# Constant products on TensorE in the eight norms of a two-block transformer kernel

## What is computed

```python
def _rmsnorm(x, g, eps=RMS_EPS):
    x32 = x.astype(jnp.float32)
    y = x32 * lax.rsqrt(jnp.mean(x32 * x32, axis=-1, keepdims=True) + eps)
    return (y * g.astype(jnp.float32)).astype(x.dtype)
...
h = rms_norm(x, norm_mlp[i]) * (1 + scale2) + shift2
x = x + gate2 * (jnp.square(jax.nn.relu(h @ mlp_w1[i])) @ mlp_w2[i])
```

## Time and profile before

| | |
|---|---|
| median of 3 runs | 3437.49 us (3431.79 to 3440.21) |
| the profiled execution, its own time | 3443.7 us |
| its span, first to last instruction | 3441.6 us |
| mean granted TensorE clock | 0.969 |
| busy share of the span: TensorE, VectorE, ScalarE, GpSimd | 94%, 57%, 36%, 37% |

### The profile page before, as it was taken

The page is one execution under the profiler, slowest core; times in us unless marked ns, Lnnn a source line. Parts: engine busy times, 40 slices in busy tenths (PEclk is TensorE's granted clock), DMA queues, the critical chain, the costliest instruction groups (busy, mean ns, idle before and its releaser), DMA issues.

```text
span 3441.6 us, 60644 instructions
## 1 busy us (share of the span) xinstructions
PE 3246.1 (94%) x24324; PEld 2497.2 (73%) x24324; DVE 1963.8 (57%) x2468; ACT 1256.1 (36%) x2203; POOL 1275.7 (37%) x729
## 2 busy tenths in 40 slices
PE   6899999999999999999999998888899999999998
PEld 4455678887776767778888776666678787578876
DVE  7457566555455555656455685555466565753345
ACT  3344431224445555531223433333322224242222
POOL 0034334444655544334443431000245443044443
PEclk9999999999999999999999999898999999999999
DMA  6433135443433433235443221000155343023322
GB/s 238 123 92 117 56 129 195 146 170 109 137 113 113 118 87 106 73 122 195 152 165 103 78 72 42 10 13 19 59 192 175 132 153 105 13 86 98 97 89 83
DMA packets 281138, 376.33 MB, mean 109 GB/s; under 512 B 59830, under 2 KB 208986, under 8 KB 269658
## 3 DMA queue, kind: packets, MB, share of 16 engines
q1 hardware_dynamic: 276568, 359.31, 33.0%
q10 hardware_dynamic: 4354, 13.98, 1.0%
HBM read 357.49 MB, written 15.73 MB: 108 GB/s over the span
## 4 chain that ended last, share of the span: by engine, by line
PE 72%; issue 9%; DVE 8%; POOL 3%; DVEq 3%; ACT 2%; DMA 0%; POOLq 0%; ACTq 0%; SPq 0%
PE ps L522 13%; PE ps L523 13%; PE ps L526 13%; PE ps L1889 2%; PE ps L1890 2%; PE ps L1891 2%; POOL w_lo L510 2%; PE ps L1094 1%; PE ps L1919 1%; PE ps L1921 1%; PE ps L1920 1%; PE ps L1929 1%; PE ps L2876 1%; DVEq L2693 1%; PE ps L2878 1%
## 5 line engine op out<-in xcount | busy, mean ns | idle before, releaser
L510 POOL TENSOR_TENSOR w_lo<-w_raw,w_hi 128x1024 fp32r<-128x1024 f32 x288 | 710.9, 2469 | 1040.3 <-ACT w_hi L501 1040.3
L522 PE MATMUL ps<-h_hi,w_hi 128*128 128x512 f32 x2304 | 907.7, 394 | 37.0 <-ACT h_hi L710 13.1
L523 PE MATMUL ps<-h_hi,w_lo 128*128 128x512 f32 x2304 | 904.6, 393 | 0.0
L526 PE MATMUL ps<-h_lo,w_hi 128*128 128x512 f32 x2304 | 826.5, 392 | 0.0
L501 ACT ACTIVATE w_hi<-w_raw 128x1024 fp32r<-128x1024 f32 x288 | 305.5, 1061 | 1100.3 <-PE ps L526 1064.7
L522 PEld LDWEIGHTS ps<-h_hi,w_hi 128*128 128x128 f32 x2304 | 437.7, 190 | 138.0 <-issue 26.1
L523 PEld LDWEIGHTS ps<-h_hi,w_lo 128*128 128x128 f32 x2304 | 437.7, 190 | 91.3
L526 PEld LDWEIGHTS ps<-h_lo,w_hi 128*128 128x128 f32 x2304 | 436.8, 190 | 91.4
L1816 POOL TENSOR_TENSOR w_lo<-w_raw,w_hi 128x512 fp32r<-128x512 f32 x208 | 270.5, 1313 | 323.0 <-ACT w_hi L2082 321.3
L864 DVE TENSOR_TENSOR h_lo<-big,h_hi 128x512 fp32r<-128x512 f32 x100 | 242.7, 2427 | 228.8 <-ACT h_hi L501 228.7
L663 DVE SCALAR_TENSOR_TENSOR big<-yT,cond,big 128x2048 f32<-128x2048 f32 x63 | 174.7, 2773 | 90.0 <-DMA yT<-in_ada_w 89.7
(11 more groups left out here) (519 smaller groups left out, 5415.2 us busy)
## 6 DMA issues: line engine op xcount, KB each, us to landing
w_raw<-in_mlp_w SPq DMA_DIRECT2D x128, 512.0 KB, 3.6
yT<-in_ada_w SPq DMA_DIRECT2D x56, 1024.0 KB, 5.8
w_raw<-in_dil_w_in SPq DMA_DIRECT2D x192, 256.0 KB, 3.0
w_raw<-in_ffn_w_up SPq DMA_DIRECT2D x176, 256.0 KB, 3.0
h_free<-in_ada_w SPq DMA_DIRECT2D x24, 1024.0 KB, 5.0
w_raw<-in_ffn_w_down SPq DMA_DIRECT2D x44, 512.0 KB, 3.6
w_raw<-in_ab_w_in SPq DMA_DIRECT2D x70, 256.0 KB, 2.9
yT<-in_ada_w SPq DMA_DIRECT2D x32, 512.0 KB, 6.2
```

The costliest lines, as they stand in the source:

```text
L510: self.nc.gpsimd.tensor_tensor(self.w_lo[:, s, :], self.w_raw[:, s, :], self.w_hi[:, s, :].bitcast(F32), ALU.subtract).then_inc(sg["w_spli ...
L522: self.nc.tensor.matmul(out, w_hi, h_hi, start=start, stop=False)
L523: self.nc.tensor.matmul(out, w_lo, h_hi, start=False, stop=False)
L526: return self.nc.tensor.matmul(out, self.w_hi[:, s, lo:lo + P], self.h_lo[:, h, :], start=False, stop=stop)
```

## The change

`norm_after` gets a helper that issues products of two constants, 128 x 128 `ones` by the 128 x 128 `ident`, in fp32, into a bank that nobody reads afterwards. They stand in TensorE's instruction order at two kinds of places, and wait for nothing themselves. One product follows each of `part(1)`, `part(2)`, `part(3)`, `part(4)` and `part(5)`, in all eight norms; seven follow line 735 in the norms without `ada` (1, 3, 5, 7 and 8). The bank is `bank + 1` for the first kind, or `bank + 2` in norm 5, and `bank` for the second.

```diff
-    def norm_after(self, block, g, layer, sub, bank, split, ada=None, ahead=None, ada_more=None, lo=None, early=0):
+    def norm_after(self, block, g, layer, sub, bank, split, ada=None, ahead=None, ada_more=None, lo=None, early=0, free=1):
...
+        def keep_clock(to, count):
+            for _ in range(count):
+                nc.tensor.matmul(self.ps[:, to % KT, 0:P], self.c["ones"][:], self.c["ident"][:], start=True, stop=True)
+
...
             for k in range(4):
                 part(k)
+                if k >= 1:
+                    keep_clock(bank + free, 1)
             if ada is not None:
...
             for k in range(4, KT - 1):
                 last = part(k)
+                if k < KT - 2:
+                    keep_clock(bank + free, 1)
             last.then_inc(sg["parts"], 1)
...
                              start=False, stop=True).then_inc(sg["sums"], 1)
-            if ada is not None:
+            if ada is None:
+                keep_clock(bank, 7)
+            else:
                 self.ada_sums(pe, ada_bank, 6, 16, ada)
...
-            k.norm_after(block, k.col("norm_g_2", KT, KT), 2, 1, 0, True, ahead=k.first_units(2), early=4)
+            k.norm_after(block, k.col("norm_g_2", KT, KT), 2, 1, 0, True, ahead=k.first_units(2), early=4, free=2)
```

## The result

The changed kernel takes 3471.24 us in the median of four runs (3467.0 to 3477.74), the kernel before 3438.72 in four: ratio 1.0108, 95% interval 1.0086 to 1.0131, so 37 us slower, or between 30 and 45; the two medians are 32.5 apart. Run again later beside other runs of the kernel before, it was 1.0103 (1.0088 to 1.0117). The forecast was 3479, in a range from 3460 to 3494.

What follows compares the result with a forecast made beforehand. TensorE, busy 94% of the span, bounds the kernel: +47.7 us in the norms' partial sums less 6 of clock won back gives +41.7, taking the median from 3437.5 to 3479, own range 3462 to 3492 (A, B and C: 3460 to 3494).

Steps and rivals of the forecast that it cites:

- Packs broken: Partial sums of each norm: full-width products turn two packs into six, four more at 0.99, 3.96 us a norm.
- The product's price: Between partial sums: each constant product costs 0.40 us, bounds 0.23 and 0.53; five are 2.0 a norm.
- Sum for the norms: First part to line 733 takes 7.94 us, plus 1.42 in norms 2, 4 and 6; all eight norms add 47.7.
- Nothing hides it: Behind line 733: engines and next stage wait in a chain, so the added time in partial sums is not hidden.
- The clock: Behind norms 1, 3, 5 and 7: the seven win back 6 us of half clock, bounds 0 and 8.4.
- The seven cost nothing: Behind line 735: seven products take 1.6 us at full clock, inside a wait of 3.27, so cost nothing.
- B: Behind the norms: the seven do not hold the clock; +47.7, 3485 us; chance 14%.
- C: Constant products between partial sums: second weight loads in the open too, 0.15 each for 40, +6, 3485 us; chance 4%.
- D: Inside the partial sums: clock falls, each norm's 7.94 grows by up to 6, 48 in eight, 3527 us; chance 4%.
- E: Partial sums: packs survive the full-width products; only 40 products count, +9.2 against -6, 3441 us; chance 9%.
- F: Partial sums: as E, but the 40 products lie in waits for squares; clock gains make it -15, 3422 us; chance 3%.

Runs made afterwards that it cites:

- the narrow products: Changed kernel with the five products between the partial sums 32 columns wide, each in the preceding part's quarter, instead of 128: ratio 0.9982 to the kernel before.
- the five in a row: Changed kernel with the same five full-width products moved together behind part 6, ahead of the full-width sum: ratio 1.0020 to the kernel before.
- the five alone: Changed kernel without the seven products behind line 735, keeping the five between the partial sums: ratio 1.0150 to the kernel before.
- the seven (or 13): 13: kernel with the seven and 128-column line 628 products, given 13 constant products for 7 (20 in norm 8, 7 in norm 6): ratio 0.9963 to before.
- the seven alone: Changed kernel without the five products between the partial sums, keeping the seven behind line 735: 3434.42 us, ratio 0.9984 to the kernel before.

## Why the prediction was right, step by step

- **Packs broken.** Forecast: two packs become six, 0.99 each. Measured 0.98 for a pack from part to constant product, in all eight norms. Shown by the timeline, and by the narrow products, which leave the packs whole.
- **The product's price.** Forecast 0.40, between 0.23 and 0.53; measured 0.42: first weight load in the open, the second beside the first stream. The forecast's reason for the order, that the products share columns, is argued and not shown: two full-width products share all of theirs, and there no load lies in the open (line 738's 1.02 behind the five in a row).
- **Sum for the norms.** 7.94 forecast and 7.95 measured where nothing else stands between; 9.36 (7.94 + 1.42) and 9.19 in norms 2, 4 and 6, since the constant product behind part 3 and line 628 are both full width and need no switch between them; the forecast had counted that switch twice. 47.7 against 47.3 in all. (The low end of one norm, given as 6.5, is 6.4 by its own terms; nothing changes by it.)
- **Nothing hides it.** Held: the five alone cost 52 us (43 to 61) in the runs, and the 47.3 that the norms grew by lies in that.
- **The clock.** Forecast: 6 of 8.4 us won back, as in three norms of four. The mechanism was right, though the forecast had no row for it and took it between its bounds. The term was undersized by the clock's rows: in all eight profiles of kernels with the seven (or 13) the clock was 1.00 behind each of norms 1, 3, 5 and 7, and in the two profiles without them (before, and the five alone) behind none. With the whole 8.4 the sum is 39, and nearer to the 37 and 35 measured. The times alone can't tell 6 from 8.4, since the seven alone won 5.5 with an interval from 1 to 10. In norms 2, 4 and 6 it stayed a loss, as forecast.
- **The seven cost nothing.** Held, and 13 would too.
- **The rivals.** B (clock not held) falls. C falls in every norm: each constant product's two weight loads start 0.11 apart, the second beside the first stream. The Trainium skill's sentence (TensorE: Matmul & The Clock Gate, Part 3: Packing small matmuls) that a weight load overlaps a matmul in flight only when their row groups differ is not what these rows show for the second load. C's price was 0.15 a product on top of the forecast's 0.40, and 0.42 was measured. D falls: the clock was 1.00 inside the partial sums even where the parts ran one by one. E falls by the timeline: packs outlive products between their parts only in the run where those are narrow. F needed the packs of E and falls with it.

The forecast was 8 us high in the median. 2.4 of it is the clock's term and 0.4 the norms'. The rest, some 5, is not told from scatter: the median of before alone was 3437.5, 3438.7, 3439.4 and 3440.3 in the sets of runs here, and the profile it was built on lay 6 above its median. The sum itself was made for a profiled span, +41.7; the two profiles of the changed kernel gave +27.4 and +37.0, so one profile alone is a poor measure of it.

## What to carry to other kernels

Narrow products in different quarters of the array's columns run side by side only as long as no full-width product stands between them in the program; filler has to go behind such a pack, or be as narrow as its parts and sit in the quarter of the part ahead of it, as in the run here. Filler that holds the clock belongs in a true wait of TensorE's queue, which the timeline shows in brackets. Where one-column products already stand in such a wait, widening them did the same here for 0.1 us in 32 records. A busy share of 94% tells nothing of either: it was 94% in both kernels.

## What the runs showed of the hardware that I had not expected

A switch from 32-column to full-width products leaves the first weight load in the open and costs about 0.2 us (0.98 for a part whose two streams take 0.88, and 1.12 where 1.02 is usual); between two full-width ones it vanishes (1.02 behind the five in a row). A product that streams 128 columns in fp32 takes nearly as long as one that streams a single column, 3.73 against 3.63 us for 32 records, yet with the one the clock stayed at 2.4 GHz over the following wait of 0.85 (2.14 in norm 6), and with the other it fell to 1.2. Products in different quarters pass one another: a narrow product started 0.9 us behind parts that are written after it. And the recurrences of the same program differed by 10 us from one profile to the next, at 0.95 against 0.93 in mean clock.
